# A hybrid attention and MoE step on one core: the layer input turned before its norm is known, and the forget gates computed behind the first projection units

## The reference, cut to what matters

```python
def _rms(x, g):
    y = xf * lax.rsqrt(jnp.mean(xf * xf, axis=-1, keepdims=True) + RMS_EPS)
    return y * g
z = hn @ w_in                      # hn = _rms(x, attn_norm)
fq, fk, fv, ff, dq, dk, dv = jnp.split(z, SPLITS, axis=-1)
fq = _rms(fq per head, fq_g)       # and fk, dq, dk; dq, dk are then rotated
logf = log_sigmoid(ff + b_forget)  # its running sum biases the fox scores
```

## Time and profile before

| | |
|---|---|
| median of 3 executions | 1354.49 us (1353.02 to 1355.77) |
| the profiled execution's own time | 1354.91 us |
| its span, first to last instruction | 1353.0 us |
| PE busy | 1288.7 us (95%) |
| DVE, ACT, POOL busy | 377.3, 209.9, 145.0 us |
| DMA | 447.06 MB, mean 330 GB/s |

### The profile page before, as it was taken

How to read it: one execution, slowest core, us unless ns; L and a number is a source line. 1 busy time by engine, 2 the same in 40 slices (tenths; PEclk the granted TensorE clock), 3 DMA queues, 4 the chain that set the end, 5 groups by cost and what they waited for, 6 DMA issues and landing times.

```text
span 1353.0 us, 16150 instructions
## 1 busy us (share of the span) xinstructions
PE 1288.7 (95%) x6083; PEld 573.3 (42%) x6084; DVE 377.3 (28%) x958; ACT 209.9 (16%) x524; POOL 145.0 (11%) x340
## 2 busy tenths in 40 slices
PE   6799999999998999999999999999999999999997
PEld 3344444565454433434344343443434344343432
DVE  3213223557252322213222121311212132121212
ACT  5111322346150101101001010100101010010100
POOL 0021300000004101011010110101011010101000
PEclk9899965579998999999999999999999999999998
DMA  8901440036525999999999999999999999999994
GB/s 286 323 29 74 174 168 1 0 128 226 209 70 210 431 427 427 428 429 429 428 430 428 428 429 429 428 428 430 428 428 430 428 429 428 430 428 427 429 426 183
DMA packets 54537, 447.06 MB, mean 330 GB/s; under 512 B 10817, under 2 KB 11090, under 8 KB 29922
## 3 DMA queue, kind: packets, MB, share of 16 engines
q1 hardware_dynamic: 54498, 446.54, 79.4%
HBM read 441.66 MB, written 4.86 MB: 330 GB/s over the span
## 4 chain that ended last, share of the span: by engine, by line
PE 65%; DMA 25%; SPq 4%; DVE 2%; POOL 1%; issue 1%; ACT 1%; DVEq 0%; POOLq 0%; ACTq 0%
DMA arena<-in_w_gate_up 23%; PE psum L1588 17%; PE psum L1556 16%; PE psum L1537 7%; PE psum L1303 5%; PE psum L1451 3%; PE psum L1407 3%; PE psum L1603 2%; PE psum L1359 2%; SPq L390 2%; PE psum L1387 1%; PE psum L1339 1%; PE psum L1571 1%; PE psum L1567 1%; PE psum L1355 1%; SPq L406 1%
## 5 line engine op out<-in xcount | busy, mean ns | idle before, releaser
L1556 PE MATMUL psum<-arena 128*64 128x512 f32 x2048 | 450.5, 599 | 18.9 <-DMA arena<-in_w_gate_up 18.4
L1556 PEld LDWEIGHTS psum<-arena 128*64 128x64 f32 x2048 | 152.9, 138 | 314.7 <-issue 314.7
L1588 PE MATMUL psum<-arena 128*64 128x512 f32 x1024 | 224.8, 597 | 0.8
L1210 DVE TENSOR_SCALAR arena<-psum 128x256 f32<-128x256 f32 x64 | 26.7, 418 | 432.4 <-PE psum L1556 430.6
L1588 PEld LDWEIGHTS psum<-arena 128*64 128x64 f32 x1024 | 78.8, 138 | 136.0 <-issue 134.6
L1303 PE MATMUL psum<-arena 128*128 128x512 f32 x288 | 127.6, 599 | 0.0
L838 ACT ACTIVATE arena<-arena 128x256 f32<-128x256 f32 x64 | 26.7, 418 | 630.5 <-DVE arena L1210 630.5
L1537 PEld LDWEIGHTS psum<-arena 128*128 128x128 f32 x768 | 88.5, 194 | 16.1 <-issue 16.1
L1537 PE MATMUL psum<-arena 128*128 128x128 f32 x768 | 91.6, 279 | 3.8 <-POOL arena L604 3.8
L1603 PE MATMUL psum<-arena 128*128 128x512 f32 x192 | 93.2, 623 | 0.0
L597 POOL COPY arena<-arena 128x6 f32 (+1 forms) x16 | 3.0, 188 | 775.6 <-PE psum L1588 703.5
(11 more groups left out here) (215 smaller groups left out, 905.2 us busy)
## 6 DMA issues: line engine op xcount, KB each, us to landing
arena<-in_w_gate_up SPq DMA_DIRECT2D x128, 2048.0 KB, 25.0
arena<-in_w_down SPq DMA_DIRECT2D x64, 2048.0 KB, 22.6
arena<-in_w_in SPq DMA_DIRECT2D x6, 2048.0 KB, 19.6
arena<-in_cache_fox_k SPq DMA_DIRECT2D x8, 512.0 KB, 3.5
arena<-in_cache_diff_k SPq DMA_DIRECT2D x8, 512.0 KB, 4.4
arena<-in_cache_fox_v SPq DMA_DIRECT2D x8, 512.0 KB, 4.0
arena<-in_cache_diff_v SPq DMA_DIRECT2D x8, 512.0 KB, 5.6
arena<-in_w_out SPq DMA_DIRECT2D x4, 1024.0 KB, 7.5
```

What stands on the lines that cost most here:

```text
L1556: last = mm(banks[n][half], XT[u][:, k, half], piece_slot(s[x])[:, c0:c0 + 512], start=False, stop=(k == 7), skip_group_check=True)
L1588: last = mm(banks[hf][half], actT[:, 4 * i + c, half], w, start=False, stop=(i == 1 and c == 3), skip_group_check=True)
```

## The change

- x tiles are transposed as they land, in the order 1, 2, 3, 0, unscaled; their squares are summed afterwards. The head norm uses `xeps` (epsilon times the row's mean square plus epsilon) in place of epsilon; v copies carry a scale.
- The constants are split: `ident` is loaded first, the rest later. The three norm vectors are issued from ACT's queue. The meta rows are loaded eight times over, to fill 128 partitions. `load_w_in(0)` becomes two halves, and it and `load_w_in(1)` move ahead of the broadcasts.
- The gate product runs behind unit 0 with its eight k-blocks in four column groups of 32; `gate_rows` sums the groups and turns them behind unit 1; exp and log move behind unit 3 on ACT; the running sum is five triangular matmuls behind unit 4, in place of the scan.

The core of the diff:

```diff
@@ -376,31 +385,41 @@
 
         @block.sync
         def _(sp):
-            sp.dma_start(xs[0][0:META], io["meta_tokens"][:, :]).then_inc(s_x[0], 16)
+            sp.dma_start(ident, io["consts"][:, 0:P]).then_inc(s_ident, 16)
             for t in range(2):
                 sp.dma_start(xs[1 + t], io["x_prompt"][0, P * t:P * (t + 1), :]).then_inc(s_x[1 + t], 16)
             sp.dma_start(xs[3], io["x_sample"].rearrange("b i n -> (b i) n")).then_inc(s_x[3], 16)
-            sp.dma_start(consts_all, io["consts"][:, :]).then_inc(s_const, 16)
-            for i, (name, n) in enumerate((("attn_norm", 8), ("ffn_norm", 8), ("diff_out_norm", 1))):
-                sp.dma_start(vecs[8 * i:8 * i + n], io[name][0].rearrange("(k p) -> k p", p=P)).then_inc(s_vec, 16)
-            sp.dma_start(gcol_x, io["ffn_norm"][0].rearrange("(p k) -> p k", p=P)).then_inc(s_gx, 16)
 
...
+            def load_first(k0, arrived):
+                c0 = BLOCKS[0][0]
+                sp.dma_start(slot(k0 // 4).rearrange("p (k n) -> p k n", k=4),
+                             io["w_in"][0, P * k0:P * (k0 + 4), c0:c0 + W].rearrange("(k p) n -> p k n", p=P)
+                             ).then_inc(arrived, 16)
+
+            load_first(0, s_win[0])
+            load_first(4, s_win0b)
+            for j in range(8):
+                sp.dma_start(xs[0][META * j:META * (j + 1)], io["meta_tokens"][:, :]).then_inc(s_x[0], 16)
+            sp.dma_start(consts_all[:, P:], io["consts"][:, P:]).then_inc(s_const, 16)
             with nc.allow_non_contiguous_dma(reason="eight columns of w_in"):
-                sp.dma_start(nb_ff[0:8, 0:1], io["b_forget"][0].rearrange("(h o) -> h o", o=1)).then_inc(s_wff, 16)
-                sp.dma_start(w_ff, io["w_in"][0, :, 1536:1544].rearrange("(k p) n -> p k n", p=P)).then_inc(s_wff, 16)
-            load_w_in(0)
+                sp.wait_ge(wff_zero, 1)
+                sp.dma_start(w_ff[:, :, 0:8], io["w_in"][0, :, 1536:1544].rearrange("(k p) n -> p k n", p=P)
+                             ).then_inc(s_wff, 16)
+            sp.dma_start(b_ff, io["b_forget"][0].partition_broadcast(P)).then_inc(s_bff, 16)
+            load_w_in(1)
+            sp.dma_start(gcol_x, io["ffn_norm"][0].rearrange("(p k) -> p k", p=P)).then_inc(s_gx, 16)
             for i, name in enumerate(("fox_q_norm", "fox_k_norm", "diff_q_norm", "diff_k_norm")):
                 sp.dma_start(gains[:, i], io[name][0].partition_broadcast(P)).then_inc(s_small, 16)
             for i, name in enumerate(("lambda_q1", "lambda_k1", "lambda_q2", "lambda_k2")):
                 sp.dma_start(lamv[:, i], io[name][0].partition_broadcast(P)).then_inc(s_small, 16)
             sp.dma_start(rot.rearrange("p t c h -> p (t c h)"), io["rot"][:, :]).then_inc(s_rot, 16)
             sp.dma_start(b_rt, io["b_router"][0].partition_broadcast(P)).then_inc(s_small, 16)
-            for bi in range(1, 6):
+            for bi in range(2, 6):
                 load_w_in(bi)
...
                     sp.wait_ge(xT_done, 4)
+                    sp.wait_ge(sq_done, 1)
                     load_cache(1, "k")
                     load_cache(1, "v")
...
-            pe.wait_ge(hnT_a, 4)
...
+            def gate_products():
+
+                pe.wait_ge(hnT_a, 4)
+                pe.wait_ge(hnT_v, 4)
+                pe.wait_ge(s_wff, 16)
+                for k in range(8):
+                    j = k % 4
+                    last = mm(banks[6][32 * j:32 * j + 32, 0:NTOK], w_ff[:, k], hnT[:, k], start=(k < 4), stop=(k >= 4))
+                last.then_inc(ff_done, 1)
+
+            def gate_rows():
+
+                pe.wait_ge(ff_copied, 1)
+                pe.wait_ge(s_const, 16)
+                for t_ in range(4):
+                    r0, n = TILES[t_]
+                    last = mm(banks[6][0:n, 448 + 8 * t_:456 + 8 * t_], ffc[:, r0:r0 + n], C["pick"], start=True, stop=True)
+                last.then_inc(ffn_done, 1)
+
+            def gate_cumulate():
+
+                pe.wait_ge(lf_ready, 1)
+                R, later = banks[6][0:8], C["cumul"][:, P:P + 1]
+                mm(R[:, 0:META], lf[0:META, 0], C["cumul"][0:META, 0:META], start=True, stop=False, skip_group_check=True)
+                mm(R[:, META:NKEY_P], lf[0:META, 0], later[0:META].to_broadcast([META, SEQ]), start=True, stop=False,
+                   skip_group_check=True)
+                mm(R[:, META:META + P], lf[:, 1], C["cumul"][:, 0:P], start=False, stop=False, skip_group_check=True)
+                mm(R[:, META + P:NKEY_P], lf[:, 1], later.to_broadcast([P, P]), start=False, stop=False,
+                   skip_group_check=True)
+                mm(R[:, META + P:NKEY_P], lf[:, 2], C["cumul"][:, 0:P], start=False, stop=True,
+                   skip_group_check=True).then_inc(ncp_done, 1)
...
+            def log_gates():
+
+                for f, i in ((ACT.Exp, 1), (ACT.Ln, 2)):
+                    ac.wait_ge(lg_v, i)
+                    nc.scalar.activation(ffl, ffl, f).then_inc(lg_a, 1)
+                    if i == 1:
+                        ac.wait_ge(lam_v, 1)
+                        nc.scalar.activation(stat[:, 10:12], stat[:, 10:12], ACT.Exp).then_inc(lam_a, 1)
+
+            ac.wait_ge(x_scale, 1)
...
-                    nc.scalar.activation(dst, z, ACT.Copy).then_inc(z_copied, 1)
+                    nc.scalar.activation(dst, z, ACT.Copy, scale=stat[rw, t:t + 1]).then_inc(z_copied, 1)
                     if t == 0:
+                if u == LOG_UNIT:
+                    log_gates()
...
+            ve.wait_ge(sq_done, 1)
+            nc.vector.tensor_scalar(stat[:, 0:4], stat[:, 0:4], 1.0 / D, EPS, ALU.mult, ALU.add).then_inc(ms_done, 1)
+            ve.wait_ge(ms_done, 1)
+            link(nc.vector.tensor_scalar(xeps, stat[:, 0:4], EPS, None, ALU.mult))
+            ve.wait_ge(rt_done, 1)
+            link(nc.vector.reciprocal(stat[:, 0:4], stat[:, 4:8]))
+            nc.vector.tensor_copy(stat[:, 9:10], stat[:, 8:9]).then_inc(x_scale, 1)
+            link(nc.vector.memset(ffv, 0.0))
...
                         pe.wait_ge(s_win[bi], 16)
+                    if u < 3:
+                        pe.wait_ge(hnT_a, max(u + 1, 2))
+                        pe.wait_ge(hnT_v, max(u + 1, 2))
...
                     for k in range(8):
+                        if u == 0 and k == 4:
+                            pe.wait_ge(s_win0b, 16)
...
+                if u == 0:
+                    gate_products()
+                if u == 1:
+                    gate_rows()
+                if u == 4:
+                    gate_cumulate()
```

More of the change, by code:

```diff
@@ L40 @@
 Y_BASE = 6
-CONSTS = [("ident", 128), ("eye4", 32), ("smask", 16), ("ones", 128), ("iota", 64), ("own", 128), ("maps", 2),
+X_ORDER = (1, 2, 3, 0)
+LOG_UNIT = 3
+CONSTS = [("ident", 128), ("eye4", 32), ("pick", 8), ("smask", 16), ("ones", 128), ("iota", 64), ("own", 128), ("maps", 2),
           ("cumul", 130), ("cumul_s", 288), ("offs", 8), ("causal", 128), ("chunk", 128)]
@@ L130, in build @@
         lf = at3(take(32), 4, 8)
-        w_ff = at3(take(64), 8, 8)
-        nb_ff = at(take(2), 2)
+        take(66)
         ncs = at(lf0, NKEY_S)
@@ L136, in build @@
         stat = at(take(48), 48)
+        xeps = stat[:, 36:40]
         nc0 = take(NKEY_P)
@@ L642, in link @@
                 ac.wait_ge(a_step, steps[0])
+            for i, (name, n) in enumerate((("attn_norm", 8), ("ffn_norm", 8), ("diff_out_norm", 1))):
+                ac.dma_start(vecs[8 * i:8 * i + n], io[name][0].rearrange("(k p) -> k p", p=P)).then_inc(s_vec, 16)
             ac.wait_ge(gain_ready, 1)
[L646 to L652, removed]
             ac.wait_ge(vec_T, 1)
@@ L655, in _ @@
             ac.wait_ge(gcol_done, 1)
-            for t in range(4):
+            for i, t in enumerate(X_ORDER):
                 r0, n = TILES[t]
-                ac.wait_ge(xT_done, t + 1)
+                ac.wait_ge(xT_done, i + 1)
                 for k in range(4):
@@ new lines, in gate_logs @@
+            def gate_logs():
+                ve.wait_ge(lg_a, 1)
+                nc.vector.tensor_scalar(ffl, ffl, 1.0, None, ALU.add).then_inc(lg_v, 1)
+                ve.wait_ge(lg_a, 2)
+                link(nc.vector.tensor_scalar(ffv, ffv, 0.0, None, ALU.min))
+                nc.vector.tensor_tensor(lf, ffv, ffl, ALU.subtract).then_inc(lf_ready, 1)
+                ve.wait_ge(lf_ready, 1)
+                nc.vector.tensor_copy(lf_new[0:META], lf[0:META, 0:1].to_broadcast([META, 8, 8])).then_inc(lf_ready, 1)
@@ L922, in _, with gate_sums @@
+            def gate_sums():
+                ve.wait_ge(ncp_done, 1)
+                nc.vector.tensor_copy(nc_p[0:8], banks[6][0:8, 0:NKEY_P]).then_inc(lf_ready, 1)
             for u, (bi, kind, g, t) in enumerate(units):
@@ L956, in _ @@
                     ve.wait_ge(z_scaled, m + 1)
+                if m == 0:
+                    gate_copy()
+                    lambdas()
                 if m == 1:
-                    ve.wait_ge(lfT_done, 1)
```

(29 more changed lines are left out.)

100 lines of the change are left out of this document (54 added, 46 removed).

## The result

The changed kernel takes 1360.32 us (median of 14 executions, 1357.59 to 1365.33) against 1354.28 us for the one before (14 executions, 1349.82 to 1355.77). The ratio is 1.0046, interval 1.0034 to 1.0057: 6.0 us slower. The profiled execution took 1359.87 us with a span of 1357.9, so 4.96 us more than the profiled one of before. That is inside the range of the prediction (1352 to 1361), 3.7 us above its forecast and in its case "slower", to which it gave 0.37. The change of 6.0 us is nearly three times the 2.1 that it forecast.

A forecast was written before the change was run, and what follows sets the result against it. Bound: PE's wait before unit 2 for unit 0's store, late in SP's queue, with 8.2 us of slack. Terms 0.5 + 1.3 + 0.35 = 2.15, taken as +2.1 on 1354.5, gave 1356.6 us; range 1352 to 1361.

The forecast's parts named there:

- case "slower": Outcome of a measured time above 1357.2 us, more than 0.2% over the kernel before; chance 0.37.
- The wait of unit 2 stands and swallows the front: PE before turning unit 2: front gains end in the wait for unit 0's store, 8.2 growing to about 15 us.
- `gate_cumulate` is on the path: PE behind unit 4: five new fp32 matmuls, after the wait where PE is busy without a gap, add 1.3 us.
- The table load before unit 6's root: ACT between unit 6's square and root: exp and log moved behind unit 3 force a table load, +0.35 us.
- The stream: SP's queue up to the store of unit 0: becomes 0.5 us longer, between ends of -4.6 and +4.6.
- rival (c): SP's queue: each small transfer costs a turn, +4.6 us on the queue, +6.3 in all, 1360.8 us; chance 0.21.
- rival (a): SP's queue: small transfers hide behind w_in(1), -4.6 us there, -3.0 in all, 1351.5 us; chance 0.18.
- all waits follow PE's own units, so the shift goes through to the end unchanged: Behind unit 6: the summed shift of 2.15 us reaches the end with nothing added or lost.
- Scaled v copies ... are one operation for one or lie in DVE's idle: Scaled v copies, `xeps` and other small moves: replaced one for one or within DVE's idle 66 to 85 us, no cost.
- the sign that the prediction named for being wrong: Some later wait (unit 5's buffer, the stores before attention) no longer follows PE.
- unit 0 can begin near 12: PE's front: with w_in(0) right behind x, unit 0 begins some 13 us earlier than 25.15; priced at nothing.
- Rival (b): PE's front: if unit 0's store is issued early enough, the 13 us reach the end, about 1343 us; chance 0.06.

The follow-up runs named there:

- the last kernel: Changed kernel with stores of units 0, 1 and 2 issued from ACT's queue, gates early, w_in(1) behind the broadcasts, meta tile turned behind unit 0: 1342.57 us.
- the first experiment: Changed kernel with the stores of units 0 and 1 issued from ACT's queue instead of behind SP's loads: 1345.57 us, ratio 0.993 to the kernel before.

## Why the prediction was right and wrong

**Right, and shown.** *The wait of unit 2 stands and swallows the front*: the release moved by 0.71 us while unit 3 ended 2.7 us sooner; doubling the gate product cost nothing, and taking the store's wait away gave 10 and 15 us. *`gate_cumulate` is on the path*: 1.34 us, forecast 1.3; with it and the table load moved ahead of the wait, release to unit 6 is 1.5 us shorter. *The table load before unit 6's root*: 0.35 us (1.91 less 1.56), forecast 0.35. The Trainium skill (ScalarE: Activation LUTs, "What ACT_TABLE_LOAD costs") would have made it some 1.7 us by its drain; the trace does not agree, the load beginning 0.02 us after the square ends. *The stream*: 0.71, forecast 0.5, rival (c)'s 4.6 and rival (a)'s -4.6 both out. That it agrees to 0.2 is in part luck, for one execution differs from another by 1.2: the release came at 62.41 and 61.17 with the old list for SP, and at 63.12, 61.94 and 62.21 with the new one, on the mean 0.6 later. Its sum has a step that does not follow, too: half of what three transfers at 0.76 us cost is 1.1 and not 1.5, which would have made the term 0.9. What it is composed of stays open; the seven meta copies are worth 0.5 to 1.6. The Trainium skill (DMA: Bandwidth & Descriptors, "Measured (HBM→SBUF, 128 partitions, SWDGE, issued from GpSimd)") would give seven transfers of 64 KB 6.7 us, an estimate from its row; leaving the seven out gave 0.5 to 1.6.

**Wrong: "all waits follow PE's own units, so the shift goes through to the end unchanged".** The terms up to unit 6 gave 2.15 and measured 2.61: 0.21 more in the stream, 0.04 in `gate_cumulate`, and 0.21 in the three units behind the wait, which took 22.25 us (8.31 and 13.94) against 22.04; the granted clock from 66 to 85 us was 0.97 there and 0.99 before. Behind it came 2.3 us more:
- *"Scaled v copies ... are one operation for one or lie in DVE's idle".* The count is one for one, but each copy, on ACT, is 0.09 us longer. At the last two v units PE follows ACT with next to no slack: 0.70 us, of which 0.6 are shown by leaving the scale out. `xeps` is named in the same sentence and is 0.06 us longer too: 0.13 us at two turnings, and what is left of the 0.70. This is also the sign that the prediction named for being wrong, a later wait that no longer follows PE. The rows of ACT at 166 to 168 us in the kernel before would have told it; the prediction did not look at them.
- 0.38 us between the first score and 300 us. The half-clock stretch begins and ends some 4 us later. Read from the trace, not tested.
- 0.45 us at the sample attention, where PE waits 1.26 us for v written out and read back, against 0.80 before:

```profile
351.48 0.99 PE L1505 MATMUL psum<-arena 128*32 128x128 f32 x24 [1.26 <-DMA arena<-out_diff_v_s]
```

```profile
347.21 0.99 PE L1418 MATMUL psum<-arena 128*32 128x128 f32 x24 [0.80 <-DMA arena<-out_diff_v_s]
```

  This wait is 0.35, 0.80 and 1.26 us in the three traces with the old front and 1.04 to 1.42 in the seven with the change, so it may be a term of some 0.4 us as well as scatter. It is not the scale, without which it was 1.42. Not tested.
- 0.6 us somewhere in the 930 us of the experts, and the last 1 us between the profiled pair (4.96) and the medians (6.0): open. Executions of one kernel lie 6 to 8 us apart; the end of the half-clock stretch in the attention is the part of that which was seen, in one pair of traces.

**Wrong, without a price: "unit 0 can begin near 12".** It began at 17.92 (the last kernel, with the meta tile out of the way, began at 11.84), because the meta tile stands before it in PE's list and waits for eight loads that stand behind both halves of w_in; it then ran at half clock up to 22.6, for half of its length (9.46 in place of 7.03 us). The prediction costed SP's list and forgot that PE's own list takes the meta tile first. So the front was worth 2.4 to 2.7 us and not 13, and the wait grew to 11.6 and not to 15. Rival (b)'s condition, a store issued early, was made true in the first experiment: it gave 1345.6, near that rival's 1343, but for another reason. 10 us of it are the wait, which the kernel before gives up just as well (1344.7), and not the front. As the front was priced at nothing, the forecast did not change by it.

**Where the number is luck.** The measured 1360.3 is, to half a microsecond, the 1360.8 of rival (c), whose mechanism (a turn for every small transfer, 4.6 us) did not happen. The time lies within 1352 to 1361, but not within the 1355 to 1359 that the prediction gave its own mechanism: the range was wide enough because it made room for rivals that are out.

In sum: forecast 2.1 on the profiled execution, measured 4.96. Of the gap of 2.9 us, 0.5 are sizes of the terms ahead of unit 6 and 0.8 the two operands read from SBUF; the other 1.6 are small shifts whose cause is open, and so is the last 1 us up to the medians.

## What to carry to other kernels

Find first the wait that swallows the gain (here a store behind 12 MB of w_in and the caches in one queue) and take it away before the work ahead of it is rebuilt: an edit of six lines was worth 10 us, the rebuilt front 2.4. Whatever a change moves to behind such a wait has its full price, so put it ahead; and when an operation gets an operand more, look along its engine's whole list for the place where somebody follows it without slack. Read the order of every engine's list against the order in which its inputs land: one small tile that comes late and stood first undid most of an early start, and moved behind unit 0 it took ACT's squares with it and did so again.

## What the hardware showed that was not expected

- The gate product, eight k-blocks over 400 columns, took 5.55 us as one group and 1.55 us with its blocks in four column groups (27.31, x16 in both): 3.6 times less, as if the four ran side by side.
- The same 256 KB stores took 6.5 us (median of two) from ACT's queue, issued at 37.5 and 45.8 us while the blocks of w_in were moving, and 7.54 us from SP's at 54.71. The gain is in when they are issued: SP's list was 17 us further back. ACT paid 0.39 us for an issue.
- PE's granted clock was 0.50 from 12.4 to 22.6 us, behind 4.81 us of transposes and in and after 7.28 us of waiting. In the last kernel, where unit 0 came 0.69 us after the transposes, the stretch from 14 to 22 us shows 1.00; there the clock fell only at 34 us, behind a wait of 1.89 us.
- The half-clock stretch of the attention lasted from 183 to 292 us in one execution and from 184 to 283 in another with the same work there, worth 4.2 us at 300 us. The two had been 0.03 us apart at the release of unit 2, so this part of the spread does not come from the front.
- An operand read from SBUF in place of a constant made a copy of 128x512 on ACT 0.09 us longer (0.60 to 0.69) and an operation of 128x8 on DVE 0.06 us longer (0.18 to 0.24).
